# Indexer key cache stored by page with channels as rows, and loaded page by page

## The chip, the cores and the metric

The kernel runs on one core of a Trainium2 chip. The metric is the time of one launch in device microseconds, the median of three runs. A profiled execution gives, for each instruction, the engine, the start and the duration; the engines are PE (TensorE, matmuls; PEld is its weight load), DVE (VectorE), ACT (ScalarE), POOL (GpSimd) and SP (SyncE, which here only issues DMAs).

## What is computed

One step of one decoder layer, for a new prompt of 512 tokens and for 8 sample sequences of 4 new tokens with 2048 cached tokens each (16 pages of 128 tokens). Norm, one input projection, an RG-LRU branch and a sparse attention branch side by side, an output projection, then a squared-ReLU MLP. The part that matters here is the indexer of the sample sequences: for every new token it scores all 2048 cached tokens and the new ones, and keeps 256 of them for attention.

```python
def _index_scores(qi, wi, ki):
    dots = jnp.einsum('...thd,...sd->...ths', qi.astype(jnp.float32), ki.astype(jnp.float32)) * (IDX_DIM ** -0.5)
    return jnp.einsum('...ths,...th->...ts', jax.nn.relu(dots), wi.astype(jnp.float32)) * (IDX_HEADS ** -0.5)

def _dsa_sample(q, k_new, v_new, qi, ki_new, wi, cache_k, cache_v, cache_kidx, page_table):
    ki_past = cache_kidx[page_table].reshape(DB, PAST_LEN, IDX_DIM)
    ki_all = jnp.concatenate([ki_past.astype(ki_new.dtype), ki_new], axis=1)
    sc = _index_scores(qi, wi, ki_all)
    sc = jnp.where(kpos[None, None, :] <= qpos[None, :, None], sc, -jnp.inf)
    _, idx = lax.top_k(sc, kk)
    ...
```

The indexer key cache has 160 pages of 128 tokens with 64 channels each (32 KB a page); 128 of the pages are used, 4.19 MB in all.

## The kernel before

Every engine runs one list of instructions in order; the order is written out by hand, and semaphores tie the lists together. The 544 tokens (512 of the prompt, 32 of the samples) lie along the columns in two halves of 272, the channels along the 128 partitions.

PE's list is the backbone: the index queries' projection (4 column blocks of 128, each 2 halves x 8 matmuls, line 1255), the index keys' and weights' projection, one block of the attention queries, the prompt's index scores (24 matmuls of line 1307), then for each of two groups of four sample sequences the index work (lines 1310 to 1334), the weighted sum over heads (line 1342), the other two query blocks, and then the key, LRU and gate projections. Two steps of the cached keys' scores (line 1360) stand behind every column block of these, 32 steps in all; then come values, attention, output projection and the MLP (line 1540).

The index work of a group. POOL gathers the group's 64 index key pages as they lie in memory, tokens as rows, with four indirect DMAs (line 425) from row numbers that DVE computes (line 988, from pt_own and keyoff). The gathered keys lie in kidx_in_sb, the first 4096 columns of arena. PE turns them in eight rounds of four 128x128 transposes into PSUM banks 4 and 5 (line 1319), ACT copies each round into kidxT (line 639, in regX), and PE waits for the last copy (kx_ev) before it makes five rounds of dot products (line 1333), which ACT rectifies into R (line 649). In group 2 a column block of the attention queries (tile_product, 32 matmuls of line 1255) comes ahead of this, and the second gather waits until the first group's transposes have read kidx_in_sb. In kidxT, pages of even number fill partitions 0 to 63 and those of odd number 64 to 127, so lines 645 and 655 write with a stride to put the scores into token order.

The chain behind it. ks_ev, the copy of the scores (lines 652 to 659), stands ahead of the next rotary copies on ACT. DVE does the prompt's top-k, then the samples' (line 1067 and 1069, 32 rounds), and in rounds 15, 21 and 28 a scan of the LRU (line 1064), for which it waits for POOL (u_rd). The LRU's next channel block starts behind that scan (lru_taps, line 678).

SP's list: the input, the first weight block, the page numbers (steps, line 340), pt_own and keyoff (lines 341 and 342), constants, the second weight block (line 350), then the cached attention keys, one DMA for each page (stream, lines 355 to 362): the register load of four page numbers (line 357), and four DMAs of 256 KB. Step 0 goes out at once; steps 1 and 2 go into arena's first 4096 columns and so wait until all 16 rounds of transposes are done (kx_tr, lines 374 and 375). The third and fourth weight blocks and so on are issued by ACT (load_block).

```python
            def stream(s, slot, landed, table, freed, uses):
                eng.load(page_regs, steps[0:1, bass.ds(s * 4, 4)])
                page = [eng.snap(r, min_val=0, max_val=NPOOL - 1) for r in page_regs]
                if freed is not None:
                    eng.wait_ge(freed, uses)
                for b4 in range(4):
                    eng.dma_start(slot[:, b4, :], table[bass.ds(page[b4], 1), :, :].rearrange("a p c -> p (a c)")).then_inc(landed, 16)
```

Of the kernel before, what the change touches and what calls it, by code (L numbers as in the profile page):

```python
# [11 lines left out]
P = 128  # L12
# [8 lines left out]
SEQ = 512  # L21
# [60 lines left out]

def build(nc, xT_d, par_d, w_in_d, w_kw_d, w_out_d, w_mlp_d, wgate_d, ck_d, cv_d, ci_d, steps_d, ptT_d,
          ident_d, rope_d, causal_d, ind_d, newmask_d, keyoff_d, yT_d, kT_d, v_d, kiT_d, lru_d):
    with ExitStack() as ctx:
# [51 lines left out]
        par = sb("par", [P, NPAR])  # L137
        keyoff = sb("keyoff", [P, 1])
        pt_own = sb("pt_own", [P, DEC_BATCH], I32)
        row_i = sb("row_i", [P, DEC_BATCH], I32)  # L140

        kw_diag = sb("kw_diag", [P, KT * 72])
# [22 lines left out]
        qz = regQ[:, 0:NH * SEQ].rearrange("p (h t) -> p h t", t=SEQ)  # L165
        kidxT = regX[:, 0:4096].rearrange("p (b c) -> p b c", b=4)
        S = regX[:, 0:GRP * NKEY].rearrange("p (g c) -> p g c", g=GRP)
# [12 lines left out]
        v_slot = [kv[:, 1], kv[:, 2], kv[:, 0]] + [wring[:, 0, i * 2048:(i + 1) * 2048].rearrange("p (b c) -> p b c", b=4) for i in range(2)]  # L180
        kidx_in_sb = arena[:, 0:4096].rearrange("p (b c) -> p b c", b=4)
        scs = carve(NKEY)[0:NS, :]
# [39 lines left out]
        w_in = [sem("w_in_even"), sem("w_in_odd")]  # L222
        kidx_in = sem("kidx_in")
        q_placed = sem("q_placed")
# [17 lines left out]
        y_pool = sem("y_pool")  # L242
        rows_rd = sem("rows_rd")
        averager_rd = sem("averager_rd")
# [14 lines left out]
        qis_rd = sem("qis_rd")  # L259
        kx_tr = sem("kx_tr")  # L260
        kx_ev = sem("kx_ev")
        kd_mm = sem("kd_mm")
# [66 lines left out]

        N_CONST = 8  # L330
        w_src = [w_in_d[i] for i in range(6)] + [w_out_d[i] for i in range(2)]

        @block.sync
        def _(eng):
# [5 lines left out]
            eng.dma_start(steps[:, :], steps_d).then_inc(steps_in, 16)  # L340
            eng.dma_start(pt_own[:, :], bass.AP(tensor=ptT_d.tensor, offset=0, ap=[[DEC_BATCH, NPG], [0, 8], [1, DEC_BATCH]])).then_inc(const_in, 16)
            eng.dma_start(keyoff[:, :], keyoff_d).then_inc(const_in, 16)
            eng.dma_start(wkw, w_kw_d).then_inc(kw_in, 16)
# [23 lines left out]
            def values(s, slot, freed, uses):  # L367
                stream(s, v_slot[slot], v_in[slot], cv_d, freed, uses)

            eng.wait_ge(steps_in, 16)  # L370


            keys(0, 2, None, 0)
            keys(1, 0, kx_tr, 16)
            keys(2, 1, kx_tr, 16)
            with eng.Fori(0, 9) as i:
# [34 lines left out]

        ci_rows = ci_d.rearrange("n (s r) d -> (n s) (r d)", r=16)

        @block.gpsimd
        def _(eng):
# [6 lines left out]

            def gather(dst, rows, index, landed):

                eng.indirect_dma_start(dst, None, rows, bass.IndirectOffsetOnAxis(ap=index, axis=0)).then_inc(landed, 16)


            nc.gpsimd.memset(regQ[:, :], 0.0)
            nc.gpsimd.memset(pTp_at[:, 0:512], 0.0)
            nc.gpsimd.memset(qbd[:, :, :, :], 0.0)  # L430
            nc.gpsimd.memset(xl[:, :, 0:3], 0.0).then_inc(zero_rd, 1)
            eng.wait_ge(rows_rd, 1)
            for b in range(4):
                gather(kidx_in_sb[:, b, :], ci_rows, row_i[:, b:b + 1], kidx_in)

# [12 lines left out]

            eng.wait_ge(kx_tr, 8)
            for b in range(4):  # L450
                gather(kidx_in_sb[:, b, :], ci_rows, row_i[:, 4 + b:5 + b], kidx_in)
            for t in range(5, 9):
# [89 lines left out]
        def _(eng):  # L542
# [91 lines left out]
            for g in range(GRP):  # L634
                for u in range(8):
                    eng.wait_ge(kx_tr, 8 * g + u + 1)
                    if g == 1 and u == 0:
                        eng.wait_ge(kd_mm, 5)
                    nc.scalar.copy(kidxT[:, u // 2, (u % 2) * 512:(u % 2) * 512 + 512], bank[4 + u % 2][:, :]).then_inc(kx_ev, 1)
                for d in range(5):  # L640
                    eng.wait_ge(kd_mm, 5 * g + d + 1)
                    b_ = bank[6 + (5 * g + d) % 2]
                    if d < 4:
                        e, ch = d // 2, d % 2
# [303 lines left out]
        def _(eng):  # L948
# [285 lines left out]
        def _(eng):  # L1234
# [75 lines left out]
            for g in range(GRP):  # L1310
                if g == 1:
                    tile_product(E_Q + 2, w, 1, hnT)
                eng.wait_ge(kidx_in, 64 * (g + 1))
                for u in range(8):
                    n = 8 * g + u
                    if n >= 2:
                        eng.wait_ge(kx_ev, n - 1)
                    for j in range(4):
                        ins = pe.transpose(bank[4 + u % 2][:, j * P:(j + 1) * P],
                                           kidx_in_sb[:, u // 2, ((u % 2) * 4 + j) * P:((u % 2) * 4 + j + 1) * P], ident[:, :])  # L1320
                    ins.then_inc(kx_tr, 1)
                eng.wait_ge(kx_ev, 8 * g + 8)
                for d in range(5):
                    n = 5 * g + d
                    if n >= 2:
                        eng.wait_ge(kd_ev, n - 1)
                    else:
                        eng.wait_ge(pi_ev, 24)
                    for b4 in range(4):
                        e, ch = (d // 2, d % 2) if d < 4 else (0, 0)  # L1330
                        rhs = kidxT[:, b4, ch * 512:ch * 512 + 512] if d < 4 else kiT[:, SEQ:NT]
                        w_ = 512 if d < 4 else NS
                        ins = pe.matmul(bank[6 + n % 2][32 * b4:32 * b4 + 32, 0:w_], qis[:, 4 * g + b4, e, :], rhs, start=True, stop=True)  # L1333
                    ins.then_inc(kd_mm, 1)
# [369 lines left out]
```

## Time and profile before

| | |
|---|---|
| median of 3 runs | 916.15 us (913.37 to 917.17) |
| profiled execution, its span | 912.3 us |
| median of the runs less that span | 3.85 us |
| PE busy | 842.3 us, 92% |
| DVE, ACT, POOL busy | 468.6, 361.0, 198.6 us |

A row of the timeline begins with start and busy time in us, then engine, line, operation, names out<-in, count, and in brackets how long the engine was idle before it and what released it. SP is all sequencer: its rows have a q, and its durations are the time that the instruction held the sequencer. "PEclk" is the granted TensorE clock as a share of full speed.

### The profile page before, as it was taken

The numbers are of one execution on the slowest core, as the hardware profiler recorded it, in microseconds if no ns is written. First come the engines' busy times: TensorE is split into PE (matmuls) and PEld (weight loads), VectorE is DVE, ScalarE is ACT, GpSimd is POOL, SyncE is SP. The second block draws the span as 40 slices with busy tenths as digits, with TensorE's granted clock in tenths as the row PEclk, the third lists the DMA queues.
The fourth block names the chain that finished last, engine by engine and source line by source line (L and its number), as shares of the span: only waits on it lengthen the run. The fifth ranks groups of instructions, "written<-read, shape, count | busy, mean of one in ns | idle before, by whom it ended". The sixth has DMA issues, their size and how long they took to land.

```text
span 912.3 us, 16428 instructions
## 1 busy us (share of the span) xinstructions
PE 842.3 (92%) x6169; PEld 694.4 (76%) x6169; DVE 468.6 (51%) x715; ACT 361.0 (40%) x771; POOL 198.6 (22%) x205
## 2 busy tenths in 40 slices
PE   5999988979999999997996899999999999999990
PEld 4864467858774455554884899999999999999990
DVE  6128999997999543321178633331122333433327
ACT  3766485335654463331243433332222333322210
POOL 2631054512333442210014211100000111100003
PEclk9999999989999989998998999999999999999995
DMA  8421405766767869994011122222222222222202
GB/s 335 158 93 41 144 13 193 258 239 215 270 218 238 293 231 381 385 379 175 0 47 47 47 92 91 74 89 93 93 92 74 88 92 92 69 93 93 92 23 98
DMA packets 52085, 133.13 MB, mean 146 GB/s; under 512 B 6113, under 2 KB 6530, under 8 KB 50754
## 3 DMA queue, kind: packets, MB, share of 16 engines
q1 hardware_dynamic: 49346, 112.98, 35.7%
q10 hardware_dynamic: 864, 10.58, 3.3%
q0 software_dynamic: 1824, 8.86, 2.6%
q8 instruction: 34, 0.56, 0.2%
q14 instruction: 17, 0.14, 0.0%
HBM read 127.74 MB, written 4.67 MB: 145 GB/s over the span
## 4 chain that ended last, share of the span: by engine, by line
PE 81%; DVE 9%; DMA 4%; ACT 3%; issue 2%; POOL 1%; SPq 1%; DVEq 0%; ACTq 0%; POOLq 0%
PE bank L1540 41%; PE bank L1255 20%; PE bank L1446 3%; DMA arena<-in_ck 3%; PE bank L1461 2%; PE bank L1360 2%; PE bank L1307 2%; DVE regM L1069 2%; DVE m L1067 2%; PE bank L1473 2%; PE bank L1398 1%; PE bank L1487 1%; DMA arena<-in_cv 1%; PE bank L1241 1%; PE bank L1333 1%
## 5 line engine op out<-in xcount | busy, mean ns | idle before, releaser
L1255 PE MATMUL bank<-regR,wring 128*128 128x272 f32 x640 | 156.8, 406 | 6.0 <-DVE regR L983 3.2
L1255 PEld LDWEIGHTS bank<-regR,wring 128*128 128x128 f32 x640 | 125.1, 197 | 34.9 <-DMA wring<-in_w_in 3.6
L1183 DVE TENSOR_TENSOR h_lo<-lx,h_hi 128x544 f32 (+1 forms) x32 | 35.8, 1120 | 111.0 <-ACT h_hi L886 110.8
L534 POOL TENSOR_TENSOR lx<-lx 128x544 f32<-128x544 f32 x30 | 32.8, 1093 | 244.6 <-ACT lx L881 244.6
L1067 DVE MAX8 m<-regM 32x8 f32<-32x2080 f32 x32 | 74.0, 2313 | 1.0
L1540 PE MATMUL bank<-h_lo,w_hi_odd 128*128 128x272 f32 x256 | 73.9, 289 | 0.0
L1540 PE MATMUL bank<-h_hi,w_hi_even 128*128 128x272 f32 x256 | 73.8, 288 | 0.0
L1540 PE MATMUL bank<-h_lo,w_hi_even 128*128 128x272 f32 x256 | 73.7, 288 | 0.0
L1540 PE MATMUL bank<-h_hi,w_hi_odd 128*128 128x272 f32 x256 | 73.7, 288 | 0.0
L1540 PE MATMUL bank<-h_hi,w_lo_odd 128*128 128x272 f32 x256 | 73.6, 287 | 0.0
L1540 PE MATMUL bank<-h_hi,w_lo_even 128*128 128x272 f32 x256 | 73.5, 287 | 0.0
L1069 DVE MATCH_REPLACE8 regM<-m,regM 32x2080 f32<-32x2080 f32 x32 | 73.5, 2297 | 0.0
L1132 DVE TENSOR_TENSOR w_lo_even<-wring,w_hi_even 128x1024 fp32r<-128x1024 f32 x31 | 38.0, 1226 | 66.1 <-ACT w_hi_even L847 66.1
L1540 PE MATMUL bank<-hn_lo,w_hi_odd 128*128 128x272 f32 x240 | 69.3, 289 | 0.0
L1540 PE MATMUL bank<-hn_hi,w_hi_even 128*128 128x272 f32 x240 | 69.3, 289 | 0.0
L1540 PE MATMUL bank<-hn_lo,w_hi_even 128*128 128x272 f32 x240 | 69.1, 288 | 0.0
L1540 PE MATMUL bank<-hn_hi,w_hi_odd 128*128 128x272 f32 x240 | 69.1, 288 | 0.0
L1540 PE MATMUL bank<-hn_hi,w_lo_odd 128*128 128x272 f32 x240 | 69.0, 287 | 0.0
L1540 PE MATMUL bank<-hn_hi,w_lo_even 128*128 128x272 f32 x240 | 69.0, 287 | 0.0
L881 ACT ACTIVATE lx<-bank 128x272 f32<-128x272 f32 x60 | 23.9, 398 | 113.5 <-PE bank L1540 113.5
L1255 PE MATMUL bank<-regM,wring 128*128 128x272 f32 x256 | 60.8, 400 | 1.8 <-ACT regM L819 1.8
L1132 DVE TENSOR_TENSOR w_lo_odd<-wring,w_hi_odd 128x1024 fp32r<-128x1024 f32 x31 | 38.1, 1230 | 44.2 <-ACT w_hi_odd L847 43.8
(249 smaller groups left out, 1800.6 us busy)
## 6 DMA issues: line engine op xcount, KB each, us to landing
arena<-in_ck SPq DMA_DIRECT2D x128, 256.0 KB, 3.9
wring<-in_w_mlp SPq DMA_DIRECT2D x64, 512.0 KB, 3.4
arena<-in_cv SPq DMA_DIRECT2D x80, 256.0 KB, 4.3
wring<-in_cv SPq DMA_DIRECT2D x48, 256.0 KB, 4.4
wring<-in_w_in ACTq DMA_DIRECT2D x4, 2048.0 KB, 9.6
wring<-in_w_in SPq DMA_DIRECT2D x2, 2048.0 KB, 14.3
regX<-in_xT SPq DMA_DIRECT2D x4, 544.0 KB, 5.7
regX<-in_xT POOLq DMA_DIRECT2D x1, 2176.0 KB, 10.3
```

What stands on the lines that cost most here:

```text
L534: nc.gpsimd.tensor_tensor(square_t[:, s, :], relu_t[:, s, :], relu_t[:, s, :], ALU.mult).then_inc(h_sq, 1)
L881: nc.scalar.activation(relu_t[:, parity, hf * HALF:(hf + 1) * HALF], bank[(2 * parity + hf) % 4][:, 0:HALF], ACT.Relu).then_inc(h_ev, 1)
L1067: vec.max(m8[0:NS, 0, :], work_s).then_inc(tk_s, 1)
L1069: vec.match_replace(work_s, m8[0:NS, 0, :], work_s, TAKEN).then_inc(tk_s, 1)
L1132: vec.tensor_tensor(w_lo[parity][:, :], w_raw[:, parity, :], w_hi[parity][:, :].bitcast(F32), ALU.subtract).then_inc(w_lo_rd, 1)
L1183: vec.tensor_tensor(h_lo[:, at], square_t[:, parity, :], h_hi[:, at].bitcast(F32), ALU.subtract).then_inc(h_lo_rd, 1)
L1255: ins = pe.matmul(bank[e % 4][0:parts, 0:HALF], lhs(k), rhs[:, k, hf * HALF:(hf + 1) * HALF], start=(k == 0), stop=(k == KT - 1))
L1307: pe.matmul(bank[6 + u % 2][:, 0:nk], qz[:, h, n * P:(n + 1) * P], kiT[:, 0:nk], start=True, stop=True).then_inc(pi_mm, 1)
L1360: ins = pe.matmul(bank[4 + s % 2][32 * b4:32 * b4 + 32, 0:P], qbd[:, 4 * (s // NPG) + b4, m, :], kv[:, slot, b4, m * P:(m + 1) * P], start ...
L1446: ins = pe.matmul(bank[2 + g][32 * b4:32 * b4 + 32, :], pT[:, g, r, 32 * b4:32 * b4 + 32], v_slot[s % V_SLOTS][:, b4, :], start=(r == 0), ...
L1461: pe.matmul(bank[4 + u % 2][:, 0:P * (n + 1)], qz[:, h, n * P:(n + 1) * P], kT[:, h // 2, 0:P * (n + 1)], start=True, stop=True).then_inc( ...
L1540: ins = pe.matmul(out, lhs[w][:, k * P:(k + 1) * P], rhs(k), start=(first and k == 0 and i == 0), stop=(last and k == KT - 1 and i == 2))
```

## The change

The index key cache is laid out by the host with channels as rows inside each page (`transpose(0, 2, 1)`, untimed). SP loads each of the 128 pages with a DMA of its own, 64 rows of 512 B, straight to its place in kidxT, in the same stretch of register load and four DMAs that the attention keys use. There are two kidxT now, one for each group, in arena and in regX. Pages 0 to 7 lie in partitions 0 to 63 and pages 8 to 15 in 64 to 127, so scores come out in token order. What falls away: the gathers on POOL, DVE's row numbers and two constants' DMAs, PE's 64 transposes, ACT's 16 copies, and the strides of two writes. On SP, group 1's pages stand ahead of step 0 of the attention keys, group 2's behind it with a wait for hn_rd (regX holds the input until then); steps 1 and 2 wait for kd_mm 5 (the first group's dot products) in place of kx_tr 16.

```diff
+        kidxT = [place[:, 0:4096].rearrange("p (b c) -> p b c", b=4) for place in (arena, regX)]
...
-            eng.dma_start(pt_own[:, :], bass.AP(tensor=ptT_d.tensor, offset=0, ap=[[DEC_BATCH, NPG], [0, 8], [1, DEC_BATCH]])).then_inc(const_in, 16)
-            eng.dma_start(keyoff[:, :], keyoff_d).then_inc(const_in, 16)
...
+            def index_keys(g, j):
+                eng.load(page_regs, steps[0:1, (g * NPG + j) * 4:(g * NPG + j + 1) * 4])
+                rows, cols = HD * (j // 8), P * (j % 8)
+                for b4 in range(4):
+                    page = eng.snap(page_regs[b4], min_val=0, max_val=NPOOL - 1)
+                    eng.dma_start(kidxT[g][rows:rows + HD, b4, cols:cols + P],
+                                  ci_d[bass.ds(page, 1), :, :].rearrange("a d k -> (a d) k")).then_inc(kidx_in[g], 16)
+
             eng.wait_ge(steps_in, 16)
+            for j in range(NPG):
+                index_keys(0, j)
 
             keys(0, 2, None, 0)
-            keys(1, 0, kx_tr, 16)
-            keys(2, 1, kx_tr, 16)
+
+            eng.wait_ge(hn_rd, 2 * KT)
+            for j in range(NPG):
+                index_keys(1, j)
+            keys(1, 0, kd_mm, 5)
+            keys(2, 1, kd_mm, 5)
...
-            eng.wait_ge(rows_rd, 1)
-            for b in range(4):
-                gather(kidx_in_sb[:, b, :], ci_rows, row_i[:, b:b + 1], kidx_in)
...
-            eng.wait_ge(kx_tr, 8)
-            for b in range(4):
-                gather(kidx_in_sb[:, b, :], ci_rows, row_i[:, 4 + b:5 + b], kidx_in)
...
             for g in range(GRP):
-                for u in range(8):
-                    eng.wait_ge(kx_tr, 8 * g + u + 1)
-                    if g == 1 and u == 0:
-                        eng.wait_ge(kd_mm, 5)
-                    nc.scalar.copy(kidxT[:, u // 2, (u % 2) * 512:(u % 2) * 512 + 512], bank[4 + u % 2][:, :]).then_inc(kx_ev, 1)
...
-                        dst = R[:, g, 0:PAST].rearrange("p (j e k) -> p e j k", e=2, k=P)[:, e, 4 * ch:4 * ch + 4, :]
-                        src = b_[:, :].rearrange("p (j k) -> p j k", k=P)
+                        dst, src = R[:, g, d * 512:(d + 1) * 512], b_[:, :]
...
-                    dst = scs[:, 0:PAST].rearrange("q (p r) -> q r p", r=16)[:, 4 * c:4 * c + 4, :]
-                    ins = nc.scalar.copy(dst, bank[4 + c % 2][0:NS, :].rearrange("q (r p) -> q r p", r=4))
+                    ins = nc.scalar.copy(scs[:, c * 512:(c + 1) * 512], bank[4 + c % 2][0:NS, :])
...
-            vec.tensor_scalar(row_i[:, :], pt_own[:, :], float(PAGE // 16), keyoff[:, 0:1], ALU.mult, ALU.add).then_inc(rows_rd, 1)
...
             for g in range(GRP):
                 if g == 1:
                     tile_product(E_Q + 2, w, 1, hnT)
-                eng.wait_ge(kidx_in, 64 * (g + 1))
-                for u in range(8):
-                    n = 8 * g + u
-                    if n >= 2:
-                        eng.wait_ge(kx_ev, n - 1)
-                    for j in range(4):
-                        ins = pe.transpose(bank[4 + u % 2][:, j * P:(j + 1) * P],
-                                           kidx_in_sb[:, u // 2, ((u % 2) * 4 + j) * P:((u % 2) * 4 + j + 1) * P], ident[:, :])
-                    ins.then_inc(kx_tr, 1)
-                eng.wait_ge(kx_ev, 8 * g + 8)
+                eng.wait_ge(kidx_in[g], 64 * NPG)
...
-                        rhs = kidxT[:, b4, ch * 512:ch * 512 + 512] if d < 4 else kiT[:, SEQ:NT]
+                        rhs = kidxT[g][:, b4, ch * 512:ch * 512 + 512] if d < 4 else kiT[:, SEQ:NT]
```

## Rows read from the trace of the kernel before

**Rows 1.** The page's chain that ended last, shares of the span by engine.

```profile
PE 81%; DVE 9%; DMA 4%; ACT 3%; issue 2%; POOL 1%; SPq 1%; DVEq 0%; ACTq 0%; POOLq 0%
```

**Rows 2.** The chain of waits from 80 to 122 us: start, us, what.

```profile
81.06 0.60 ACT arena L632
...
86.67 3.83 PE bank L1333 x40
90.51 7.53 PE bank L1255 x32
...
103.63 3.75 PE bank L1333 x32
```

**Rows 3.** Groups by line from 80.8 to 108.2 us.

```profile
L1319 PE MATMUL bank<-ident,arena 128*128 128x128 f32 x64 | 8.9, 283 | 1.3 <-ACT regX L639 1.3
L639 ACT COPY regX<-bank 128x512 f32<-128x512 f32 x16 | 8.6, 587 | 8.9 <-PE bank L1319 8.9
```

**Rows 4.** Timeline of ACT and PE at the scores' copy.

```profile
115.24 1.02 ACT L656 COPY arena<-bank 32x512 f32<-32x512 f32 x1 [0.69 <-PE bank L1342]
...
118.12 1.22 PE L1255 MATMUL bank<-regR,wring 128*128 128x272 f32 x3 [2.79 <-ACT lx L588]
```

**Rows 5.** DVE's timeline at the three scans inside the samples' top-k.

```profile
219.99 1.29 DVE L1064 TENSOR_TENSOR_SCAN arena<-lx 128x544 f32<-128x544 f32 x1 [6.47 <-POOL lx L484]
...
252.47 1.29 DVE L1064 TENSOR_TENSOR_SCAN arena<-lx 128x544 f32<-128x544 f32 x1 [2.78 <-POOL lx L484]
...
286.95 1.29 DVE L1064 TENSOR_TENSOR_SCAN arena<-lx 128x544 f32<-128x544 f32 x1
```

**Rows 6.** SP's timeline: key step 1, and its last issue with step 2's first.

```profile
103.12 1.88 SPq L362 DMA_DIRECT2D arena<-in_ck  x4
104.67 1.32 SPq L362 DMA_DIRECT2D arena<-in_ck  x2
```

**Rows 7.** SP's instructions by line: durations ns min/median/max, first and last start us.

```profile
L357 SPq TENSOR_LOAD <-steps x4: 299/303/502, 13.8 to 107.9; - x4
L358 SPq FUSED_REGOPS  x64: 96/118/161, 14.4 to 405.1; - x64
L362 SPq FUSED_REGOPS  x108: 37/37/42, 145.8 to 289.3; - x108
L362 SPq DMA_DIRECT2D arena<-in_ck x108: 332/333/1407, 146.0 to 289.5; - x108
L345 SPq DMA_DIRECT2D ident<-in_ident x1: 432/432/432, 6.4 to 6.4; - x1
L340 SPq DMA_DIRECT2D steps<-in_steps x1: 376/376/376, 3.5 to 3.5; - x1
```

**Rows 8.** Instruction fetches: DMA queues of 0 to 120 us, and SP from 145.9 to 147.8.

```profile
q8 instruction: 4, 0.07, 0.2%
...
q8 instruction: 1, 0.02, 3.5%
L362 SPq DMA_DIRECT2D arena<-in_ck x2: 333/730/1128, 146.0 to 146.5; - x2
```

**Rows 9.** The output's eight stores of 272 KB (line 408), issue to landing.

```profile
DMA to landing us min/median/max: 2.1/2.1/2.4
```

**Rows 10.** PE's timeline around an idle stretch, and the granted clock behind it (windows).

```profile
176.48 7.60 PE L1255 MATMUL bank<-regR,wring 128*128 128x272 f32 x32
184.01 1.08 PE L1360 MATMUL bank<-arena,qbd 128*32 128x128 f32 x32
191.17 1.93 PE L1360 MATMUL bank<-arena,qbd 128*32 128x128 f32 x32 [6.08 <-DMA arena<-in_ck]
193.03 9.64 PE L1255 MATMUL bank<-regR,wring 128*128 128x272 f32 x32
191.20:195.20 4.00, 4.00 (x37) 3.05 (x38) 3.93 (x4) 2.01 (x5) 0.00 (x0) 0.50 1.06 394
```

**Rows 11.** DMA queues from 70 to 102 us: packets, MB, share (the second gather).

```profile
q0 software_dynamic: 576, 2.10, 20.1%
```

More of the change, by code:

```diff
@@ L80, with build @@
 SCAN_ROUNDS = (15, 21, 28)
-def build(nc, xT_d, par_d, w_in_d, w_kw_d, w_out_d, w_mlp_d, wgate_d, ck_d, cv_d, ci_d, steps_d, ptT_d,
-          ident_d, rope_d, causal_d, ind_d, newmask_d, keyoff_d, yT_d, kT_d, v_d, kiT_d, lru_d):
+def build(nc, xT_d, par_d, w_in_d, w_kw_d, w_out_d, w_mlp_d, wgate_d, ck_d, cv_d, ci_d, steps_d,
+          ident_d, rope_d, causal_d, ind_d, newmask_d, yT_d, kT_d, v_d, kiT_d, lru_d):
     with ExitStack() as ctx:
@@ L137, in build @@
         par = sb("par", [P, NPAR])
-        keyoff = sb("keyoff", [P, 1])
-        pt_own = sb("pt_own", [P, DEC_BATCH], I32)
-        row_i = sb("row_i", [P, DEC_BATCH], I32)
         kw_diag = sb("kw_diag", [P, KT * 72])
@@ L165, in build @@
         qz = regQ[:, 0:NH * SEQ].rearrange("p (h t) -> p h t", t=SEQ)
-        kidxT = regX[:, 0:4096].rearrange("p (b c) -> p b c", b=4)
         S = regX[:, 0:GRP * NKEY].rearrange("p (g c) -> p g c", g=GRP)
@@ L180, in build @@
         v_slot = [kv[:, 1], kv[:, 2], kv[:, 0]] + [wring[:, 0, i * 2048:(i + 1) * 2048].rearrange("p (b c) -> p b c", b=4) for i in range(2)]
-        kidx_in_sb = arena[:, 0:4096].rearrange("p (b c) -> p b c", b=4)
+        kidxT = [place[:, 0:4096].rearrange("p (b c) -> p b c", b=4) for place in (arena, regX)]
         scs = carve(NKEY)[0:NS, :]
@@ L222, in build @@
         w_in = [sem("w_in_even"), sem("w_in_odd")]
-        kidx_in = sem("kidx_in")
+        kidx_in = [sem(f"kidx_in{g}") for g in range(GRP)]
         q_placed = sem("q_placed")
@@ L242, in build @@
         y_pool = sem("y_pool")
-        rows_rd = sem("rows_rd")
         averager_rd = sem("averager_rd")
@@ L259, in build @@
         qis_rd = sem("qis_rd")
-        kx_tr = sem("kx_tr")
-        kx_ev = sem("kx_ev")
         kd_mm = sem("kd_mm")
@@ L328, in build @@
         block = ctx.enter_context(nc.Block())
-        N_CONST = 8
+        N_CONST = 6
         w_src = [w_in_d[i] for i in range(6)] + [w_out_d[i] for i in range(2)]
@@ L410, in _ @@
             eng.wait_ge(stored, 16 * KT)
-        ci_rows = ci_d.rearrange("n (s r) d -> (n s) (r d)", r=16)
         @block.gpsimd
@@ L421, in link @@
                 eng.wait_ge(pool_step, steps[0])
-            def gather(dst, rows, index, landed):
-                eng.indirect_dma_start(dst, None, rows, bass.IndirectOffsetOnAxis(ap=index, axis=0)).then_inc(landed, 16)
             nc.gpsimd.memset(regQ[:, :], 0.0)
@@ L643, in _ @@
                     if d < 4:
-                        e, ch = d // 2, d % 2
-                        dst = R[:, g, 0:PAST].rearrange("p (j e k) -> p e j k", e=2, k=P)[:, e, 4 * ch:4 * ch + 4, :]
-                        src = b_[:, :].rearrange("p (j k) -> p j k", k=P)
+                        dst, src = R[:, g, d * 512:(d + 1) * 512], b_[:, :]
                     else:
@@ L1672 @@
     newmask = np.where((qb[:, None] == qb[None, :]) & (qt[None, :] <= qt[:, None]), 0.0, OUT_OF_REACH).astype(f4)
-    keyoff = (q[:, None] % 8).astype(f4)
+    ci = a["ci"][0].transpose(0, 2, 1)
     steps = np.asarray(page_table).reshape(GRP, 4, NPG).transpose(0, 2, 1).reshape(1, KSTEPS * 4)
@@ L1680 @@
         "w_mlp": w_mlp, "wgate": wgate,
-        "ck": ck, "cv": a["cv"][0].reshape(NPOOL, PAGE, WIDTH), "ci": a["ci"][0], "steps": steps, "ptT": np.asarray(page_table).T,
-        "ident": np.eye(P, dtype=f4), "rope": rope, "causal": causal, "ind": ind, "newmask": newmask, "keyoff": keyoff,
+        "ck": ck, "cv": a["cv"][0].reshape(NPOOL, PAGE, WIDTH), "ci": ci, "steps": steps,
+        "ident": np.eye(P, dtype=f4), "rope": rope, "causal": causal, "ind": ind, "newmask": newmask,
     }
```

## Prediction

> **What bounds the kernel now.** I read the chain that ended last first. PE holds 81% of it and DMA 4% [rows 1], so a cut counts where PE works or waits. The same chain in order of time shows the index stage as a strict alternation. From the end of ACT's last rectified prompt score (81.06 + 0.60 = 81.66) to the first dot product at 86.67 there are only transposes and ACT's copies; the dots take 3.84 us up to 90.51, the query block 7.53; then transposes again until 103.63, where the second group's dots begin [rows 2]. In the groups by line the two halves of the alternation are 64 transposes, 8.9 us, and 16 copies, 8.6 us [rows 3]. Each waits for the other, so the stage pays the sum of the latencies and neither sum alone.
>
> Then I asked who else waits later. DVE runs the top-k without a gap except at the scans: it waits 6.47 us for POOL in the first, 2.78 in the second and not at all in the third [rows 5]. DVE starts its top-k from the prompt's scores, which the change leaves where they are, so these two waits, 9.25 us, are all that an earlier PE can take out of DVE's list ahead of the third scan. Behind that scan the last LRU block begins, and PE waits for it. More than 9.2 us cannot reach the end.
>
> Last I read SP, which after key step 0 only waits until key step 1 goes out at 103.12 [rows 6], and gets 128 new DMAs in that time.
>
> **What is removed.** Without transposes and copies, group 1's dots start at 81.7 in place of 86.67, and end 3.84 later at 85.5. The query block takes 7.53, so PE stands ready for group 2's dots at 93.1 in place of 103.63: 10.5 us earlier, provided the pages are there [rows 2]. The strided copy of the scores, 1.02 us [rows 4], becomes a contiguous one; the nearest row is a copy of 512 columns at 0.59 [rows 3], so the last copy ends 0.4 us earlier, and PE waits for what ACT does next (2.79 us for line 588, [rows 4]): 0.4 us on the path. The other three of those copies lie beside PE and give nothing, as do DVE's row numbers, POOL's gathers (POOL is idle on both sides of the second four) and the two constants' DMAs. The rectified writes of line 649 lose a stride but keep their length and lie beside the dots.
>
> **What is added, all of it on SP.** A page is one DMA instruction. In a quiet stretch four issues take 1.88 us, so from start to start (1.88 - 0.333) / 3 = 0.516 us; across the next register load it is 1.32 - 0.333 = 0.987 us [rows 6, 7]. A step of four pages costs 3 x 0.516 + 0.987 = 2.535 us. Does a smaller DMA issue faster? A DMA of one row holds SP for 376 ns, one of 128 rows 432 [rows 7]; 64 rows lie between, so I take the key pages' own 333 ns, and at most a few hundredths less.
>
> SP starts when the page numbers have landed, at 13.8 [rows 7]; that DMA is queued behind the first weight block, and nothing ahead of it changes. Then come 16 steps for group 1, key step 0, and 16 for group 2, 33 in all. The first register load is 0.2 us longer than the rest [rows 7]. Group 1 is issued by 13.8 + 0.2 + 16 x 2.535 = 54.6, 27 us before PE wants it at 81.7: hidden, and it stays so if every issue costs half as much again. Group 2 is issued by 13.8 + 0.2 + 33 x 2.535 = 97.7, already 4.6 us after PE wants it at 93.1.
>
> To this come fetches of instructions. In the 108 key issues between 145 and 290 us the median is 333 ns but the longest 1407 [rows 7], and the one of 1128 ns stands in a stretch of 1.9 us in which the instruction queue moved a packet of 16 KB [rows 8]. That queue shows four such packets in the first 120 us [rows 8]; at 0.8 us each (1128 - 333) I take 3.2 us, with bounds of 0 and, since the unrolled list of SP is longer itself, 6.4. And the last DMA has to land: a store of 272 KB takes 2.1 us from issue to landing [rows 9]; for 32 KB I take 2.0 from an issue that starts 0.4 before the end. So group 2 is complete at 97.7 + 3.2 - 0.4 + 2.0 = 102.5, 1.1 us before the dots of now.
>
> **What that does to PE.** It idles from 93.1 to 102.5, 9.4 us. The nearest row is the idle stretch of 6.08 us ahead of 191.17: 32 matmuls behind it took 1.93 us against 1.08 just before it, and the next column block 9.64 against 7.60; the granted clock in the 4 us behind it was 0.50, the lower level, 1.2 GHz [rows 10]. That is 0.85 + 2.04 = 2.9 us lost. In the kernel before, the dots follow transposes closely; with the change they follow an idle stretch, so I charge them the 2.9. Bounds: 0 if PE waits less than about a microsecond, 2.9 at most.
>
> **Waits that are moved.** SP's wait for hn_rd has everything behind it (group 2, all attention keys), but SP reaches it at about 57 us, when PE has long used all of that norm in its projections: no cost; so too the wait for kd_mm 5, due at 85.5 and reached at about 101. Key steps 1 and 2 go out from 101 to 106 in place of 103 to 108 [rows 6], and PE uses them only behind line 1342 and two more query blocks of 7.53 us each [rows 2]: covered by 15 us and more. The kidx_in wait on PE has the whole backbone behind it; ACT's rotary copies, POOL and through them the LRU wait for that, and so the delay goes to the end one to one.
>
> **Sum.** Landing 102.5 against 103.63: -1.1; lower clock: +2.9; shorter copy: -0.4. Together +1.4 us: span 912.3 + 1.4 = 913.7. The median lies 916.15 - 912.3 = 3.85 above the profiled span, so 917.6. About 0.5%, 4.6 us, is what a measurement of this kernel can tell from no change; this is inside it.
>
> **The rivals.** (1) The pages come in time and the gain shows. Its mechanism is that issue is not what limits them: the 64 pages of a group are 2.10 MB, which the second gather moves within the same 70 to 102 us, mostly idle, stretch [rows 11], and if SP's register work (37 ns for an address, 96 to 161 for four page numbers) is fused and the 64-row DMAs go out faster, a step of 2.35 us is enough to land at 13.8 + 0.2 + 33 x 2.35 + 1.6 = 93.2. Then PE gains 10.5 + 0.4 and DVE's two waits let 9.2 through: 903.1, or 906.9 as a median. It decides from a landing before about 97. Against it: 0.333 us of each 0.516 is the DMA instruction itself, the same for every one of 108 pages [rows 7].
>
> The Trainium skill ("DMA: Bandwidth & Descriptors", section "Issuing engines are not separate DMA queues") says that the time a sequencer takes to initiate a DMA is usually small relative to the DMA itself. By that rule this rival would be the forecast. The rows here stand against it for pages this small.
>
> (2) Slower. Each page number is now taken from its register right ahead of its DMA. If that is an instruction of its own, four of 37 ns with as much again between them replace one of 118 [rows 7]: + 4 x 0.075 - 0.15 = +0.15 a step. With 6.4 us of fetches, group 2 lands at 13.8 + 0.2 + 33 x 2.685 + 6.4 + 1.6 = 110.6, and the sum is 7.0 + 2.9 - 0.4 = +9.5: 921.8, as a median 925.7. The place is PE's wait for kidx_in[1]; the sum turns positive from a landing at 101.1, and passes 4.6 us at 105.7. For it: 128 issues in a row, so that every 0.1 us more per issue is 13 us. Against it: the quiet rows are very even.
>
> (3) The change is without effect because the pages of group 1 come late as well: it would need 27 us more, twice the issue time of now. I give it nothing of its own.
>
> **How the numbers follow.** Landing between 97 and 105.7 is the forecast, chance 0.54; rival 1 has 0.20, rival 2 has 0.26. These are the chances of the same, faster and slower. The forecast's own range is 911.6 to 920.7; to leave out no more than 2 in 10 it is widened to half of rival 1, 908, and most of rival 2, 925.
>
> **What would show it.** The lines of the transposes and of ACT's copies are gone, and group 1's dots start near 81.7. SP shows 128 issues from about 14 to 101 us with step times near 2.5 us. PE's longest new wait is for a DMA from in_ci, from 93 on for some 9 us, and the dots behind it take about twice their 3.7 us, with a granted clock of 0.5. In DVE the waits ahead of the scans stay near 6.5 and 2.8 us. If instead these two are gone, rival 1 holds; if they grow by several us, rival 2. I am wrong in kind if PE's wait there is short, in size if the time of an issue differs from 0.516 us.

## The result, and the profile after

| kernel | median us | profiled span us |
| --- | --- | --- |
| before, same chip | 915.91 | 912.3 |
| changed | 933.33 | 930.4 |

The ratio is 1.0184, with a 95% interval of 1.0139 to 1.0228: the changed kernel is slower by 17 us. 917.6 was forecast, with a range up to 925.

The page's chain of the changed kernel, shares by engine and by line. It answers [rows 1].

```profile
PE 65%; SPq 13%; DVE 9%; DMA 5%; issue 5%; ACT 3%; POOL 1%; DVEq 0%; ACTq 0%; POOLq 0%
PE bank L1513 40%; PE bank L1237 13%; SPq L366 7%; SPq L353 4%; PE bank L1333 2%; DMA arena<-in_ck 2%; PE bank L1419 2%; DVE regM L1051 2%; DVE m L1049 2%; PE bank L1371 1%; DMA steps<-in_steps 1%; PE bank L1434 1%; SPq L362 1%; DMA arena<-in_cv 1%; DVE lx L955 1%
```

SP's queue has risen from 1% of the chain to 13%. Two lines carry it: L366, the page DMAs of the index keys, and L353, the loads of the attention's keys and values. Both turn out to matter.

SP's timeline, first stretch. It answers [rows 6].

```profile
14.40 49.20 SPq L366 DMA_DIRECT2D arena<-in_ci  x64
64.22 2.19 SPq L353 DMA_DIRECT2D arena<-in_ck  x4
66.94 47.30 SPq L366 DMA_DIRECT2D regX<-in_ci  x64
114.92 5.41 SPq L353 DMA_DIRECT2D arena<-in_ck  x8
```

The same instructions by line (ns min/median/max, first and last start), and their time from issue to landing. They answer [rows 7, 9].

```profile
L366 SPq DMA_DIRECT2D regX<-in_ci x64: 468/469/512, 66.9 to 113.8; - x64
...
DMA to landing us min/median/max: 1.9/2.0/9.0
```

A page of index keys holds SP for 469 ns, not for the 333 of a page of attention keys. Start to start that is 0.66 us within a step and 0.98 across a register load, so a step of four pages takes 3 x 0.66 + 0.98 = 2.96 us. The last page is issued at 113.8 and lands at 115.8.

PE's timeline behind the prompt's scores. It answers [rows 2].

```profile
81.89 3.83 PE L1306 MATMUL bank<-arena 128*32 128x512 f32 x40 [0.78 <-ACT arena L623]
85.65 7.60 PE L1237 MATMUL bank<-regR,wring 128*128 128x272 f32 x32
115.78 5.71 PE L1306 MATMUL bank<-regX,arena 128*32 128x512 f32 x32 [22.54 <-DMA regX<-in_ci]
...
122.31 7.18 PE L1315 MATMUL bank<-regM,wm 128*32 128x512 f32 x20 [0.68 <-ACT regM L633]
131.94 1.41 PE L1237 MATMUL bank<-regR,wring 128*128 128x272 f32 x5 [2.45 <-ACT lx L579]
```

Group 1's dots start 4.8 us earlier than before. Group 2's wait 22.54 us for the pages and start 12.2 us later than before. The granted clock falls in the wait to 0.50, the lower of its levels (1.2 GHz), as the windows show (us; busy time of PE, PEld, DVE, ACT, POOL; granted clock; DMA share; GB/s). They answer the last row of [rows 10].

```profile
96.10:115.70 19.60, 0.00 (x0) 0.00 (x0) 19.36 (x57) 0.00 (x0) 0.00 (x0) 0.50 0.16 45
115.78:121.49 5.71, 5.71 (x40) 1.32 (x40) 5.64 (x18) 1.79 (x3) 0.00 (x0) 0.63 0.92 277
```

So the dots take 5.71 us for 3.75. While SP issues the pages the DMA engines are busy for 0.16 of the time only: the issue is the limit, not the transfer. ACT's copy of the scores is shorter, and PE waits for ACT 2.45 us in place of 2.79 [rows 4]:

```profile
124.25 0.57 ACT L639 COPY arena<-bank 32x512 f32<-32x512 f32 x1 [1.99 <-PE bank L1315]
```

At the query block of 131.94 the kernel is 13.8 us late (118.12 before, [rows 4]). DVE's timeline at the scans takes this up as a longer wait ahead of the first scan; [rows 5] has waits of 6.47 and 2.78:

```profile
233.87 1.29 DVE L1046 TENSOR_TENSOR_SCAN arena<-lx 128x544 f32<-128x544 f32 x1 [18.24 <-POOL lx L475]
266.10 1.29 DVE L1046 TENSOR_TENSOR_SCAN arena<-lx 128x544 f32<-128x544 f32 x1 [2.53 <-POOL lx L475]
...
300.59 1.29 DVE L1046 TENSOR_TENSOR_SCAN arena<-lx 128x544 f32<-128x544 f32 x1
```

The third scan, the last of these, comes 13.6 us late and the end 18.1. Most of the 4.5 us between is lost at the end of the value stage, where PE multiplies the probabilities with the pages of values. PE's timeline there, changed kernel:

```profile
425.34 1.06 PE L1419 MATMUL bank<-wring,regR 128*32 128x512 f32 x8 [1.44 <-DMA wring<-in_cv]
...
428.08 1.07 PE L1419 MATMUL bank<-wring,regR 128*32 128x512 f32 x8 [0.65 <-DMA wring<-in_cv]
430.74 1.94 PE L1419 MATMUL bank<-arena,regR 128*32 128x512 f32 x8 [1.59 <-DMA arena<-in_cv]
433.32 1.93 PE L1419 MATMUL bank<-arena,regR 128*32 128x512 f32 x8 [0.65 <-DMA arena<-in_cv]
435.19 1.93 PE L1423 MATMUL bank<-arena,regR 32*32 32x512 f32 x8
```

And the kernel before at the same place:

```profile
414.14 1.06 PE L1446 MATMUL bank<-arena,regR 128*32 128x512 f32 x8 [1.32 <-DMA arena<-in_cv]
416.83 1.06 PE L1446 MATMUL bank<-arena,regR 128*32 128x512 f32 x8 [1.62 <-DMA arena<-in_cv]
417.82 1.06 PE L1450 MATMUL bank<-arena,regR 32*32 32x512 f32 x8
```

Waits for values of 4.3 us stand against 2.9, and the last three groups of products run at half the rate (1.93 us for 1.06, together 2.6 us more). That is 4.0 us more, and it was in no step of the prediction.

A second transfer lies over these pages, POOL's load of the input. The profile page of the changed kernel has it as

```profile
regX<-in_xT POOLq DMA_DIRECT2D x1, 2176.0 KB, 11.0
```

It is issued at 412.55 us and lands at 423.5, and its queue takes 48.3% of the DMA engines' time in between. The four steps of pages that SP issues from 412.2 on land from 425.3 on, the first of them 13.1 us after its issue, where the profile page gives these DMAs a median of 4.1. The kernel before has the same load (issued at 398.45) over its last four steps. So the waits at the end of the stage have two possible sources, SP's pace and these shared engines.

### The profile page after: what moved, and what is told of

Read it like the earlier page. It is cut to its first block, busy times and chain, and to the rows that moved or that the text cites. A ratio compares the mean times of both kernels' runs of the same rounds, so it can differ in the third digit from the quotient of the medians.

```text
span 930.4 us, 16686 instructions
## 1 busy us (share of the span) xinstructions
PE 835.8 (90%) x6105; PEld 686.9 (74%) x6105; DVE 470.4 (51%) x714; ACT 350.7 (38%) x755; POOL 193.2 (21%) x197
## 4 chain that ended last, share of the span: by engine, by line
PE 65%; SPq 13%; DVE 9%; DMA 5%; issue 5%; ACT 3%; POOL 1%; DVEq 0%; ACTq 0%; POOLq 0%
PE bank L1513 40%; PE bank L1237 13%; SPq L366 7%; SPq L353 4%; PE bank L1333 2%; DMA arena<-in_ck 2%; PE bank L1419 2%; DVE regM L1051 2%; DVE m L1049 2%; PE bank L1371 1%; DMA steps<-in_steps 1%; PE bank L1434 1%; SPq L362 1%; DMA arena<-in_cv 1%; DVE lx L955 1%
## 5 line engine op out<-in xcount | busy, mean ns | idle before, releaser
L1237 PE MATMUL bank<-regR,wring 128*128 128x272 f32 x640 | 152.0, 397 | 6.8 <-DVE regR L966 4.3
L1237 PEld LDWEIGHTS bank<-regR,wring 128*128 128x128 f32 x640 | 121.5, 192 | 34.5 <-issue 5.7
```

Source lines behind the costliest of these rows:

```text
L1237: ins = pe.matmul(bank[e % 4][0:parts, 0:HALF], lhs(k), rhs[:, k, hf * HALF:(hf + 1) * HALF], start=(k == 0), stop=(k == KT - 1))
```

## Experiments

My theory after the result: the page DMA's own issue time makes group 2 late, and all of the prediction stands but that term. Its rival for the size: the transfers or their form cost the time. For the 4 us at the value stage the question was whether SP's pace or the DMA engines' set them.

### What an issue costs: e1_probe

The kernel before, with 26 DMAs of seven shapes put into SP's idle stretch; they write into a tile that is free there.

```diff
+for i in range(4):
+    eng.dma_start(regM[64 * (i % 2):64 * (i % 2) + 64, ...], ci_64[bass.ds(page[i], 1), :, :].rearrange("a d k -> (a d) k")).then_inc(probed, 16)
 ...
+for i in range(4):
+    eng.dma_start(regM[:, 768 + 64 * i:768 + 64 * i + 64], ci_d[bass.ds(page[i], 1), :, :].rearrange("a p c -> p (a c)")).then_inc(probed, 16)
```

> The kernel before, with 26 DMAs of seven shapes added to SP's idle stretch behind key step 0 (into regM, which nothing uses until 81 us). It measures the disputed cost, how long one DMA instruction holds SP, by itself: a page DMA of the changed kernel takes 469 ns, a key DMA 333. Theory 'rows': a DMA over 64 partitions takes 469 ns and one over 128 takes 333, whatever the bytes of a row and the way the rows are written. Theory 'bytes': 512 B rows take 469, 2 KB rows 333, on 64 or 128 partitions, and 256 B rows more than 469. Theory 'form': the shapes in which the page index is merged with the row ('(a d) k') take 469, those with the row first ('p (a c)') take 333, at any size. Time unchanged within 5 us of before.

Measured 919.18 us in one execution, 3.3 above the kernel before on the same chip: the probe disturbs little, as expected. SP's timeline; each line is one shape, in the order 64 rows x 512 B (the page's axis merged with the rows, as in the change), the same (merged with the columns), 128 x 256 B (with the rows), the same (with the columns), 64 x 2 KB, 128 x 2 KB, 128 x 512 B:

```profile
16.69 2.49 SPq L379 DMA_DIRECT2D regM<-in_ci  x4
19.28 2.64 SPq L382 DMA_DIRECT2D regM<-in_ci  x4
22.01 2.05 SPq L385 DMA_DIRECT2D regM<-in_ci  x4
24.16 1.80 SPq L388 DMA_DIRECT2D regM<-in_ci  x4
26.14 2.92 SPq L391 DMA_DIRECT2D regM<-in_ck  x4
29.16 1.00 SPq L394 DMA_DIRECT2D regM<-in_ck  x2
30.25 2.01 SPq L397 DMA_DIRECT2D regM<-in_ck  x4
```

Four DMAs on 64 partitions take 2.5 us and more, four on 128 partitions about 1.8 to 2.0, whether a row has 256 B, 512 B or 2 KB. So neither the bytes nor the size of a row makes the price; the number of partitions (here also the number of rows) goes with it, and 64 cost more than 128. That is no rule down to one: the DMA of a single row in [rows 7] took 376 ns, and the one of 128 rows there 432. The form adds on 64 partitions: by the trace's durations a single instruction took 468 ns with the page's axis merged with the rows and 545 with the columns. On 128 partitions both forms took 381 or 382 at their shortest; in the loads of the attention it is 333. Why 381 and 333 differ was not found.

### Without group 2's pages: e2_one_group

SP loads group 1 only, and the second group's dots read group 1's keys. This takes the wait away with its cause.

```diff
-            for j in range(NPG):
-                index_keys(1, j)
-            keys(1, 0, kd_mm, 5)
+            keys(1, 0, kd_mm, 10)
 ...
-                eng.wait_ge(kidx_in[g], 64 * NPG)
+                eng.wait_ge(kidx_in[0], 64 * NPG)
 ...
-                        rhs = kidxT[g][:, b4, ch * 512:ch * 512 + 512] if d < 4 else kiT[:, SEQ:NT]
+                        rhs = kidxT[0][:, b4, ch * 512:ch * 512 + 512] if d < 4 else kiT[:, SEQ:NT]
```

> The changed kernel without its second group of 64 index page DMAs: the second group's dot products read the first group's keys (so the second group's scores are of the wrong keys), and key steps 1 and 2 wait for both groups' dots. It takes away the lateness and keeps every other part. Theory 'late pages' (the 18 us are PE's wait for group 2, and without it the gain is what DVE's two waits let through): 915.9 - 9.2 = 906.7, DVE waits no longer ahead of the first two scans. Rival 'later stage' (the 4 us that the changed kernel loses after 320 us are the change's own): 906.7 + 4 = 911. Rival 'no gain' (something behind gives the 10 us back): 914 to 917.

Measured 913.54 us, ratio 0.9976 (0.9952 to 1.0001). PE's timeline:

```profile
85.17 3.83 PE L1304 MATMUL bank<-arena 128*32 128x512 f32 x40 [0.78 <-ACT arena L621]
...
96.45 3.71 PE L1304 MATMUL bank<-arena 128*32 128x512 f32 x32
```

The second group's dots follow the query block without a wait and at full rate: the 20 us against the changed kernel are those pages. But against the kernel before little is gained: the 906.7 us of the first theory did not come, although the dots start 7.2 us earlier. Part of that lies ahead of the dots in this profile. Group 1's dots start 3.3 us later than in the changed kernel, with the same wait for ACT ahead of them, as the granted clock was lower in the early projections. The window from 64 to 72 us has it (columns as above); in the changed kernel its clock is 1.00:

```profile
64.00:72.00 8.00, 6.97 (x21) 4.20 (x22) 4.72 (x13) 4.63 (x20) 0.00 (x0) 0.79 0.57 157
```

The profile of e3 has this stretch too. Whether it belongs to the edits or to the executions, and whether all ten executions of e2 had it, is not shown. The rest is given back behind the scans. Where, e4 and e7 tell.

### Pages of 128 rows: e3_rows128

The same pages, same bytes, same number of DMAs; a page lies as 128 rows of 256 B, and the rectified scores are written with a stride again to suit.

```diff
-                rows, cols = HD * (j // 8), P * (j % 8)
+                cols = HD * j
 ...
-                    eng.dma_start(kidxT[g][rows:rows + HD, b4, cols:cols + P],
-                                  ci_d[bass.ds(page, 1), :, :].rearrange("a d k -> (a d) k")).then_inc(kidx_in[g], 16)
+                    eng.dma_start(kidxT[g][:, b4, cols:cols + HD],
+                                  ci_d[bass.ds(page, 1), :, :].rearrange("a p c -> p (a c)")).then_inc(kidx_in[g], 16)
 ...
-    ci = a["ci"][0].transpose(0, 2, 1)
+    ci = a["ci"][0].reshape(NPOOL, 2, HD, HD).transpose(0, 1, 3, 2).reshape(NPOOL, P, HD)
```

> The changed kernel with each page laid out as 128 rows of 256 B (two halves of 64 tokens by 64 channels) in place of 64 rows of 512 B, so that a page DMA spans 128 partitions and is written row first; the rectified write has a stride again. All else as changed. Theories 'rows' and 'form': the issue falls to 333 ns, a step to 2.5 us, group 2 lands near 102 and PE's wait there falls from 22.5 to about 9 us: 933.3 - 13 = 920. Theory 'bytes': the issue stays at 469 ns or grows, 933 or more.

Measured 914.1 us, ratio 0.9986 (0.996 to 1.0013). SP's issues by line, then PE's timeline at the second group's dots, and DVE's at the third scan:

```profile
L366 SPq DMA_DIRECT2D regX<-in_ci x64: 332/333/1365, 57.5 to 98.4; - x64
```

```profile
100.19 5.34 PE L1308 MATMUL bank<-regX,arena 128*32 128x512 f32 x32 [3.50 <-DMA regX<-in_ci]
```

```profile
281.27 1.29 DVE L1048 TENSOR_TENSOR_SCAN arena<-lx 128x544 f32<-128x544 f32 x1
```

Only the shape of the DMA is changed (with the write that suits it), the issue is 333 ns again, the last page comes 15.4 us sooner, and the time falls by 19 us to that of the kernel before. More came back than the 13 us that were expected. A step of four pages takes 2.42 us, less than the 2.5 of the expectation, and DVE waits for POOL at none of the three scans, so the third starts 19.3 us sooner than in the changed kernel; from there on nearly nothing is added (19.6 at the end).

In time this is what the prediction forecast (landing 102.5, no difference that can be measured); the run has it at 100.2. The path is another. The prediction kept DVE's waits of 6.5 and 2.8 us, and here they are gone and the third scan is 5.7 us ahead of the kernel before, but the end only 1.5. As in e2, group 1's dots start some 3.4 us late, so against the rest of the kernel the landing counts as one at about 96.8, on rival 1's side of its 97.

### The key step moved behind the pages: e8_order

The changed kernel with its 64-row pages; only the order on SP differs.

```diff
-            keys(0, 2, None, 0)
-
             eng.wait_ge(hn_rd, 2 * KT)
             for j in range(NPG):
                 index_keys(1, j)
+
+            keys(0, 2, None, 0)
```

> The changed kernel with one edit: the first key step (4 DMAs of in_ck) is issued behind group 2's pages instead of ahead of them; pages stay 64 rows of 512 B. That takes 2.7 us off SP's way to group 2's last page. Theory (the dots start when that page lands, and what follows moves one for one): last page at 113.0 in place of 115.7 us, first key scores, the scans and the end 2.7 us sooner: 930.6 us. Rival (the key step, now issued at 112 us, comes late for the first key scores at 159 us): no, 47 us lie between; so if the time does not fall, something other than the landing sets it.

Measured 929.98 us, ratio 1.0131 (1.0059 to 1.0203); the changed kernel, on the same chip beside it, 930.4. In time the 2.7 us can't be told from nothing. PE's timeline has them:

```profile
114.19 5.68 PE L1306 MATMUL bank<-regX,arena 128*32 128x512 f32 x32 [20.02 <-DMA regX<-in_ci]
```

The dots start 1.6 us ahead of the first profile of the changed kernel and 2.4 ahead of the second. The profiled execution lost it again later, under a mean granted clock of 0.951 against 0.959. That the dots follow the landing is shown; that the end does, by these 2 us, is not.

### The changed kernel again: after_again

> The changed kernel once more, for a second profile. Theory (SP's stalls in the value loop are a property of the kernel, since its SP runs there without slack): the value stage again adds 2 to 4 us to the shift of 13.6 us, with waits of over 3 us for in_cv at its end. Rival (the half clock at the end of the value stage in the first profile was one execution's): the wait is there but the last products take 1.06 us, and the stage adds 1.5 us. 931 to 935 us in either case.

Measured 930.4 us, a little under what was expected, ratio 1.0158 (1.0087 to 1.023), profiled span 927.0. PE's timeline at the dots and at the end of the value stage:

```profile
116.54 5.41 PE L1306 MATMUL bank<-regX,arena 128*32 128x512 f32 x32 [23.23 <-DMA regX<-in_ci]
...
422.51 1.07 PE L1419 MATMUL bank<-wring,regR 128*32 128x512 f32 x8 [0.70 <-DMA wring<-in_cv]
...
424.98 1.06 PE L1419 MATMUL bank<-wring,regR 128*32 128x512 f32 x8 [0.38 <-DMA wring<-in_cv]
427.69 1.06 PE L1419 MATMUL bank<-arena,regR 128*32 128x512 f32 x8 [1.65 <-DMA arena<-in_cv]
430.32 1.71 PE L1419 MATMUL bank<-arena,regR 128*32 128x512 f32 x8 [1.56 <-DMA arena<-in_cv]
```

The loss at the end of the value stage is there again: four waits, 4.3 us, and the last products at the lower rate. Two profiles agree that it belongs to the kernel. Its size does not: from the third scan to the end it is 2.9 us here and 4.5 in the first profile. In the chain SP's queue has 10% here in place of 13, with 7% again at L366 but 1% at L353.

### Is SP's pace the limit of the value stage? e5_values20 and e6_after_values20

One edit, in the kernel before (e5) and in the changed one (e6): one register load brings the page numbers of five value steps, in place of one load a step.

```diff
                 for j in range(V_SLOTS):
-                    values(i * V_SLOTS + (V_SLOTS + j), j, v_mm, i * V_SLOTS + (j + 1))
+                    eng.wait_ge(v_mm, i * V_SLOTS + (j + 1))
+                    for b4 in range(4):
+                        page = eng.snap(lap_regs[4 * j + b4], min_val=0, max_val=NPOOL - 1)
+                        eng.dma_start(v_slot[j][:, b4, :], cv_d[bass.ds(page, 1), :, :].rearrange("a p c -> p (a c)")).then_inc(v_in[j], 16)
```

with `eng.load(lap_regs, ...)` of 20 registers ahead of this loop, once for five steps.

> The kernel before with one edit on SP's value loop: one register load of 20 page numbers per turn of five steps, in place of five loads of 4. SP's turn falls from 13.3 us by 4 x 0.5 = 2 us. Theory SP (the value stage is fed at the pace of SP's issues, 2.66 us a step without a wait): the steps come at about 2.25 us until a buffer is wanted, and TensorE's two waits at the end of the stage (1.32 + 1.62 = 2.9 us for in_cv) go: 913 us. Rival DMA (the 16 DMA engines are full in this stage: share 1.02 to 1.05, 376 to 409 GB/s): SP issues sooner, the pages land no sooner, the waits stay: 916 us.

> The changed kernel with the same one edit on SP's value loop and nothing else. Its value stage loses 4 us more than that of before: waits for in_cv of 1.44 + 0.65 + 1.59 + 0.65 = 4.3 us (before 2.9), and the last three groups of products at half the clock (1.94 us for 1.06). Theory SP: these waits go, and with them the half clock: 933.3 - 4.3 - 2.6 = 926.4 us. Rival DMA (the engines are full): 933 us. Either way the 13.6 us lost at the index keys' dots stay.

e5: 916.57 us, ratio 0.9975 (0.9944 to 1.0006). e6: 928.36 us, ratio 1.0127 (1.0075 to 1.0178), where the changed kernel had 1.0184 and 1.0158. SP's waits from 330 to 430 us (us in total, times, longest), first the changed kernel:

```profile
SPq L353 <- PE bank L1419: 19.4, 1, 19.4
```

Then e6:

```profile
SPq L396 <- PE bank L1424: 25.9, 9, 19.2
```

PE's timeline of e6 at the end of the stage:

```profile
426.78 1.06 PE L1424 MATMUL bank<-arena,regR 128*32 128x512 f32 x8 [0.49 <-DMA arena<-in_cv]
429.22 1.07 PE L1424 MATMUL bank<-arena,regR 128*32 128x512 f32 x8 [1.38 <-DMA arena<-in_cv]
```

In the changed kernel SP waits once, at the loop's first step, and never behind it: it issues without a pause, so whatever holds it up makes the pages later. In e6 it waits eight more times, 6.7 us in all, for a buffer, so it has slack; the four waits of 4.3 us shrink to two of 1.9, and the last products run at full rate. In the stretches of 10 us from 360 to 410 the DMA engines move 355 to 381 GB/s in the changed kernel and 387 in all five in e6: SP kept them a little short, though a share of 1.02 (400 to 420 us) looks full. That shows SP's part in the 4 us. In time e6 lies 2 to 5 us below the changed kernel, with intervals that overlap, and above the 926.4 of the theory.

It does not clear the DMA engines. At 387 GB/s the 1.05 MB of a step take 2.7 us, as long as SP needs to issue one without a stall (2.66), and in e6 too POOL's load shares the engines with the last steps. In the kernel before, the rival's forecast came true: the same edit brings nothing. SP then has the same slack (eight more waits, 6.7 us), but the last two waits for values stay (1.09 and 1.54 us). The shared engines would explain these; no run moves POOL's load, so it is not shown.

### All together: e4_behind and e7_both

e4 is e3 with 16 page numbers a load, and with the key step behind group 2. e7 is e4 with the edit on the value loop.

```diff
-            def index_keys(g, j):
-                eng.load(page_regs, steps[0:1, (g * NPG + j) * 4:(g * NPG + j + 1) * 4])
+            def index_keys(g, q):
+                eng.load(four_regs, steps[0:1, (g * NPG + 4 * q) * 4:(g * NPG + 4 * q + 4) * 4])
+                for i in range(16):
 ...
-            keys(0, 2, None, 0)
-
             eng.wait_ge(hn_rd, 2 * KT)
 ...
+            for q in range(NPG // 4):
+                index_keys(1, q)
+            keys(0, 2, None, 0)
```

> The changed kernel with three edits: a page is 128 rows of 256 B, as in the run before; one register load serves 16 page DMAs in place of 4; the first key step (4 DMAs of in_ck) is issued behind group 2's pages. Theory (the dots wait for group 2's last page and for nothing else): SP needs 64 x 0.52 + 4 x 0.7 = 36 us a group, so the last page lands at 14.6 + 72 + 2 = 89 us, ahead of TensorE's 93; the wait of 3.50 us at the dots and the half clock behind it (5.34 us for 3.8) are gone. The samples' scans then end as in the run without group 2's pages, 5.8 us ahead of before, and the value stage gives part of it back, as there: 911 to 914 us. Rival A (nothing is given back): 906.7 us by the scans' own length. Rival B (16 registers in one load take 4 times as long as 4, 1.2 us): the last page lands at 91 us, still in time, same result. Rival C (the wait was not what cost): 914, as the run with 128 rows.

> Both edits together: 128-row pages, 16 registers a load, the first key step behind them, and 20 registers a turn in the value loop. Theory SP: the gain at the dots is carried through the value stage: 907 to 910 us. Rival DMA: as without the value edit, 911 to 914 us. Rival (something behind the value stage takes the place: the weights of the output projection and of the MLP come no sooner): the value products end 5 to 6 us ahead of before and the time is 912 to 914 all the same.

e4: 912.53 us, ratio 0.9942 (0.9921 to 0.9963). e7: 908.68 us, ratio 0.9906 (0.9873 to 0.9939). The dots and the end of the value stage in PE's timeline, first of e4:

```profile
94.33 3.71 PE L1309 MATMUL bank<-regX,arena 128*32 128x512 f32 x32 [1.22 <-DMA regX<-in_ci]
...
409.32 1.63 PE L1422 MATMUL bank<-arena,regR 128*32 128x512 f32 x8 [1.65 <-DMA arena<-in_cv]
411.90 1.94 PE L1422 MATMUL bank<-arena,regR 128*32 128x512 f32 x8 [0.96 <-DMA arena<-in_cv]
```

Then of e7:

```profile
93.95 3.71 PE L1314 MATMUL bank<-regX,arena 128*32 128x512 f32 x32 [0.73 <-DMA regX<-in_ci]
...
404.62 1.07 PE L1427 MATMUL bank<-arena,regR 128*32 128x512 f32 x8 [0.82 <-DMA arena<-in_cv]
407.17 1.06 PE L1427 MATMUL bank<-arena,regR 128*32 128x512 f32 x8 [1.48 <-DMA arena<-in_cv]
```

And DVE's timeline of e7 at the third scan, which starts there without a wait, as the two ahead of it do:

```profile
277.82 1.29 DVE L1054 TENSOR_TENSOR_SCAN arena<-lx 128x544 f32<-128x544 f32 x1
```

In both kernels PE waits about 1 us for the pages, the dots run at full rate and DVE's waits at the scans are gone. The third scan of e7 starts at 277.82 in place of 286.95 [rows 5], 9.1 us sooner. In e4, where the scan starts at 277.70, the value loop takes about half of that back: its last products start at 411.90 in place of 416.83, 4.9 us sooner, and run at the lower rate. In e7, which differs from e4 by the edit on the value loop alone, they start 9.7 us sooner, and the time is 0.94% below the kernel before. It is faster than both kernels; against e4 it gains 3.9 us, with intervals that overlap. What the longer register load and the moved key step bring each, e4 does not tell apart.

## Why the prediction was wrong

**The step that failed** is the price of a page's issue. It took "the key pages' own 333 ns, and at most a few hundredths less" from DMAs on 128 partitions, as if fewer rows could only be cheaper; two setup DMAs of one row and of 128 rows stood for the ends [rows 7]. On 64 partitions the issue takes 469 ns, 0.136 more, so 0.54 us more a step. The register work became 0.12 us a step shorter: in e3, where an issue is 333 ns again, SP's issues are 0.85 us apart across a register load, where the sum has 0.987, and 0.52 within a step, as in the sum. So a step takes 2.96 us in place of 2.535; times 32 that is 13.6 us, and the landing moves from 102.5 to 115.8, by 13.3. The prediction had named this sign itself: wrong in size if the time of an issue differs from 0.516 us. With the measured step in it, its sum gives +14.9 us and 931.1 as a median; 933.33 and 930.4 were measured. That this comes so close is in part luck, for the sum has 0.9 us too much for the clock and nothing for the value stage. e3, which changes the shape alone, shows the reverse.

**What held.** Group 1 is hidden: its pages are issued by 63.6, and its dots start at 81.89 (81.7 predicted). The fetches of instructions cost SP 3.2 us in the prediction; what SP lost over the medians of its steps is 2.3 + 0.5 us in the two groups and some 0.4 in the key step between. Landing takes 2.0 us, as taken. The wait stands where it was put, at the dots of group 2, and the moved waits cost nothing. The copy gave 0.34 us (0.4 predicted).

**What was off by less.** The lower clock cost 2.0 us at the dots, not 2.9: what came behind them, line 1315, took 7.18 us as before. The register work that rival 2 went by changed the other way, by -0.12 us a step for its +0.15; the 0.98 us across a load only looks like the 0.987 of the sum, as 0.136 of it is the longer issue. So rival 2 had the place and the sign, and the sentence that every 0.1 us an issue is 13 us, but not the cause.

**What was missing.** "The delay goes to the end one to one" holds up to the third scan (13.6 us) and not behind it: 18.1 us at the end. In the second profile it is 11.8 at the scan and 14.7 at the end. SP has no slack in the value stage, so a stall of SP there is not caught up; e6 and e7, where it has slack, lose less. Whether POOL's load on the same engines costs the rest was not tested. Why SP has more stalls in the changed kernel's value loop was not settled either. Of its long issues there five begin within 0.7 us of a packet of 16 KB on the instruction queue, as in [rows 8]. The longest, 1815 ns at 418.6 against the median of 333, has none of these beside it, only one of 8 KB on another instruction queue; its cause stays open.

**Rival 1** was wrong for this change, since the issue is what limits the pages. It was right on what it needs (a step short enough that the pages land by about 97) and on the cap: 9.2 us, and 9.1 measured at e7's third scan. It put the median at 906.9; e7 has 908.68, and e4, without the edit on the value loop, 912.53.

The Trainium skill ("DMA: Bandwidth & Descriptors", section "Issuing engines are not separate DMA queues"), which calls the time to initiate a DMA usually small relative to the DMA itself, does not describe these pages: 64 of them took SP 47.30 us, and from 96.1 to 115.7 us the DMA engines were busy for 0.16 of the time.

## What to carry to other kernels

When a gather becomes many small DMAs, price the instruction that issues one by a DMA of the same number of partitions, and multiply by the count before anything else: here 0.14 us an issue came to 17 us over 128 pages, and the second group started 12 us late. Then try the layout in which a small DMA covers all 128 partitions, and put what isn't urgent behind them. Where a queue feeds a stage with no wait of its own in it, it has no slack: its stalls are not caught up there, and part of the time won ahead of that stage is lost in it again (e4). Loading the page numbers for many DMAs at once gave it slack in e6 and e7.

## What the runs showed of the hardware

- The same 32 KB took 469 ns to issue as 64 rows of 512 B and 333 as 128 rows of 256 B. More bytes a row changed little: in e1, 64 rows of 2 KB took 468 to 493 ns.
- A register load costs a little less by the register when it brings many: 4 took 0.30 us [rows 7], 16 and 20 took 0.98 and 1.21, so 75, 61 and 60 ns each, by SP's instructions of e4 and then of e7:

```profile
L364 SPq TENSOR_LOAD <-steps x8: 972/978/1180, 13.8 to 83.6; - x8
```

```profile
L393 SPq TENSOR_LOAD <-steps x5: 1195/1206/1212, 305.0 to 375.9; - x5
```

Across a load of 4, SP's issues were 0.85 us apart in e3, across one of 16 they were 1.52 in e4, and 0.52 without one. So for 16 pages one load saves 0.3 us against four.
- Stretches at the lower clock come at other places in another execution of the same kernel. In the first profile of the changed kernel the granted clock is 0.50 from 157.7 to 164.3 us and 1.00 from 133.7 to 137.0; in the second it is the other way round. In e2 and e3 such stretches stand with a loss of some 3 us ahead of the dots. A difference of that size between two single profiles means nothing until such stretches have been looked for in both.
